# Ring sizes and asking distance of the expert gathers; the last norm's rows moved onto the scores; spread weights read with step zero

## The reference, cut to what matters

```python
hpre = jnp.einsum('tkd,td->tk', u_tab[e_b], x_b)
y = jnp.einsum('tk,tkd->td', g_b * jax.nn.gelu(hpre, approximate=False), v_tab[e_b])
x2 = layer_norm(DN_ALPHA * x1 + y, ln2_g, ln2_b)
```

## Time and profile before

| | us |
|---|---|
| runs, median of 3 | 2384.51 |
| runs, lowest and highest | 2361.98, 2390.08 |
| profiled execution, its own time | 2363.84 |
| its span, first to last instruction | 2362.0 |
| expert loop, first to last dot product | 559.8 to 2333.7 |
| busy share PE, DVE, ACT, POOL | 71%, 58%, 17%, 43% |
| moved by DMA in all | 719.97 MB |
| of it by GpSimd's queue | 556.16 MB |
| mean granted TensorE clock | 0.774 of 2.4 GHz |

### The profile page before, as it was taken

How to read it: one execution, slowest core, us unless ns; L and a number is a source line. 1 busy time by engine, 2 the same in 40 slices (tenths; PEclk the granted TensorE clock), 3 DMA queues, 4 the chain that set the end, 5 groups by cost and what they waited for, 6 DMA issues and landing times. The chain is left out here.

```text
span 2362.0 us, 32086 instructions
## 1 busy us (share of the span) xinstructions
PE 1668.0 (71%) x12789; PEld 1004.3 (43%) x12789; DVE 1362.1 (58%) x2926; ACT 393.5 (17%) x745; POOL 1024.4 (43%) x1094
## 2 busy tenths in 40 slices
PE   7998878874878784787776657867785555555554
PEld 7886756752556451465444324544451001000000
DVE  4394367576444458755434777454457666575744
ACT  1331422131222011123101102320001001000000
POOL 0000200003544445464544545445556666666664
PEclk9997989995999895698887869988886555555555
DMA  9215366427999999699999998999999999999996
GB/s 258 54 36 178 94 160 215 169 89 254 360 356 394 396 370 360 231 348 376 388 385 337 366 352 300 343 354 379 368 389 347 364 354 360 362 369 371 378 370 256
DMA packets 270871, 719.97 MB, mean 305 GB/s; under 512 B 29219, under 2 KB 77822, under 8 KB 269690
## 3 DMA queue, kind: packets, MB, share of 16 engines
q0 software_dynamic: 152336, 556.16, 63.6%
q1 hardware_dynamic: 115736, 160.91, 20.2%
q10 hardware_dynamic: 2650, 0.85, 0.2%
HBM read 696.10 MB, written 21.82 MB: 304 GB/s over the span
## 5 line engine op out<-in xcount | busy, mean ns | idle before, releaser
L2448 DVE CUSTOM_DVE_ANT_0 arena<-arena,ps 128x1024 f32<-128x1024 f32 x520 | 634.4, 1220 | 577.5 <-PE ps L2501 548.5
L2381 POOL DMA_INDIRECT arena<-peer_u_dram,arena x520 | 503.3, 968 | 656.7 <-DVE arena L2448 553.7
L2514 PE MATMUL ps<-arena 128*32 128x512 f32 x2080 | 404.6, 862 | 287.1 <-DMA arena<-peer_v_dram,arena 275.9
L2386 POOL DMA_INDIRECT arena<-peer_v_dram,arena x520 | 491.4, 945 | 166.7 <-issue 152.0
L1291 PE MATMUL ps<-arena 128*128 128x128 f32 (+1 forms) x3072 | 444.8, 303 | 61.6 <-DMA arena<-w_in_dram 29.4
L1291 PEld LDWEIGHTS ps<-arena 128*128 128x128 f32 x3072 | 406.8, 211 | 179.9 <-issue 158.4
L2501 PE MATMUL ps<-arena 48*128 48x512 bf16 x1040 | 260.4, 494 | 262.2 <-DVE arena L2448 242.4
L2501 PEld LDWEIGHTS ps<-arena 48*128 48x128 bf16 x1040 | 53.2, 97 | 544.5 <-DVE arena L2448 384.0
L2514 PEld LDWEIGHTS ps<-arena 128*32 128x32 f32 x2080 | 51.2, 126 | 380.5 <-issue 303.4
L2482 ACT ACTIVATE arena<-arena 128x4 f32<-128x4 f32 x130 | 26.7, 205 | 935.4 <-DVE arena L2448 935.1
L383 PE MATMUL ps<-arena 128*128 128x260 f32 (+1 forms) x704 | 131.0, 348 | 4.1 <-ACT arena L461 4.1
(11 more groups left out here) (363 smaller groups left out, 1830.8 us busy)
## 6 DMA issues: line engine op xcount, KB each, us to landing
arena<-w_in_dram SPq DMA_DIRECT2D x40, 1024.0 KB, 10.9
arena<-peer_wq_dram SPq DMA_DIRECT2D x32, 1024.0 KB, 11.6
arena<-w_out_dram SPq DMA_DIRECT2D x16, 1024.0 KB, 10.5
arena<-w_in_dram SPq DMA_DIRECT2D x30, 512.0 KB, 3.9
arena<-peer_u_dram,arena POOLq DMA_INDIRECT x520
arena<-peer_v_dram,arena POOLq DMA_INDIRECT x520
arena<-w_branch_a_dram SPq DMA_DIRECT2D x8, 1024.0 KB, 10.2
arena<-w_branch_b_dram SPq DMA_DIRECT2D x8, 1024.0 KB, 11.0
```

Of the source, the lines that this page charges most:

```text
L2381: pool.indirect_dma_start(e["U"][:, k % RU, :], None, a["peer_u"][0], offsets(k)).then_inc(u_in[k % RU // UB], 16)
L2386: pool.indirect_dma_start(e["V"][:, j % RV, :], None, a["peer_v"][0], offsets(j)).then_inc(v_in[j % RV // BATCH], 16)
L2448: dve.tensor_tensor_reduce(u, u, ps[:, 0:2, :], 1.0, 0.0, ALU.mult, ALU.add, e["hp"][:, c:c + 1]).then_inc(sem("e_h"), 1)
L2514: mm = pe.matmul(ps[32 * c:32 * c + 32, b + h, :], e["hz"][:, (k + c) % RH, ZW // 2 - r:ZW // 2 - r + 32], e["V"][:, (k + c) % RV, h * 512 ...
```

## The change

The U ring goes from 8 rows to 6, the V ring from 8 to 12, and LAG from 14 steps to 9. `y` lies over the first half of the scores, and `pick` keeps one column for each of the 16 tokens, which TensorE reads 128 times with step zero. The rows of block n-1 are loaded for the norm at step 118 of that block, once the next choice is done, with a semaphore of its own for the sample; scores for block 2 and 3 and for the sample wait until `y` has been saved. The sample's scores go from step 386 to 404, and its choice from 1.5 to 1.2 steps a piece.

```diff
--- before.py
+++ after.py
@@ -145,7 +145,7 @@
     _F_AT[f"s{_g}"], _F_AT[f"se{_g}"] = 74.7 + 4.4 * _g, 75.0 + 4.4 * _g
 BEGINS = (-160.0, 3.0, 106.0, 224.0)
 STRETCH = (1.0, 1.0, 1.3, 1.3)
-CHOOSE_PACE = (0.55, 0.58, 0.78, 0.94, 1.5)
+CHOOSE_PACE = (0.55, 0.58, 0.78, 0.94, 1.2)
 RECUR_SPAN = 31.0
 SLOTS = 3
 
@@ -1395,6 +1395,8 @@
     def scored(g):
         yield front_at(n, f"se{g}")
         wait("s", g + 1)
+        if n > 1 and g == 0:
+            act.wait_ge(m["sem"]("y_saved"), 16 * (n - 1))
         act.activation(d["scores"][:, 4 * g:4 * g + 4].rearrange("p j n -> p (j n)"), ps[:, FB, :], ACT.Copy).then_inc(F_["se"], 1)
 
     yield from gates(0)
@@ -2148,8 +2150,8 @@
             turn_chosen(m, pe, d)
 
 
-RU, RV, RH = 8, 8, 12
-LAG, LEAD = 14, 12
+RU, RV, RH = 6, 12, 12
+LAG, LEAD = 9, 12
 GROUP = 16
 UB = 2
 ZW = 63
@@ -2158,12 +2160,13 @@
 
 def running_buffers(m, space):
     take = space.take
-    m["e"] = dict(U=take([P, RU, D]), V=take([P, RV, D]), hz=take([P, RH, ZW]), pick=take([P, GROUP, P], BF16), pick1=take([P, GROUP]),
+    m["e"] = dict(U=take([P, RU, D]), V=take([P, RV, D]), hz=take([P, RH, ZW]), pick=take([P, GROUP], BF16), pick1=take([P, GROUP]),
                   xp=take([P, 2, 512], BF16), hp=take([P, 2 * GROUP]), hg=take([P, 2, BATCH]), g2=take([P, D]), b2=take([P, D]),
-                  y=take([P, D]), stat=take([P, 4]))
+                  stat=take([P, 4]))
     f = dict(choose={name: take(shape, dt) for name, shape, dt in CHOOSE}, scores=take([P, HP, NK]))
     m["e"]["junk"] = f["choose"]["one"].rearrange("p h i j -> p (h i j)")
     m["finbuf"] = take([P, NFIN * (P + NS)])
+    m["e"]["y"] = flat(f["scores"])[:, 0:D]
     at = space.at
     m["b1"] = {name: take(shape) for name, shape in (
         ("PR", [P, HR, 4, 64]), ("TTr", [P, HR, 64]), ("TMr", [P, HR, 64]), ("Xr", [P, HR, 64]), ("Vt", [P, 512]), ("Kt", [P, 512]),
@@ -2207,7 +2210,7 @@
     return 2 if n < NT else FB
 
 
-SS = 386.0
+SS = 404.0
 
 
 def rows_pe(m, pe):
@@ -2239,6 +2242,7 @@
         yield SS + 0.6 + half
         act.wait_ge(sem("ss_mm"), half + 2)
         act.wait_ge(sem("sel_done"), 2 * NT)
+        act.wait_ge(sem("y_saved"), 16 * (NT - 1))
         act.activation(d["scores"][0:NS, 8 * half:8 * half + 8].rearrange("p (b j) n -> p b (j n)", b=2), ps[0:NS, FB:FB + 2, :], ACT.Copy
                        ).then_inc(sem("ss_out"), 1)
     for q in range(3):
@@ -2321,13 +2325,13 @@
 
     def load_x(n):
         for here, x, _ in rows(n):
-            sp.dma_start(here, x).then_inc(sem("e_x"), 16)
+            sp.dma_start(here, x).then_inc(sem("e_x" if n < NT else "e_xs"), 16)
 
     def save(n):
         sp.wait_ge(sem("e_y"), n + 1)
         for here, _, out in rows(n):
-            sp.dma_start(out, here).then_inc(saved, 16)
-            m["saved"] += 16
+            sp.dma_start(out, here).then_inc(sem("y_saved") if n < NT else saved, 16)
+            m["saved"] += 16 * (n == NT)
 
     yield -2.0
     sp.wait_ge(sem("e_zeroed"), 2)
@@ -2346,12 +2350,12 @@
         if k == 2 * GROUP:
             sp.dma_start(e["g2"], a["ln2_g"].to_broadcast([P, D])).then_inc(sem("e_gb"), 16)
             sp.dma_start(e["b2"], a["ln2_b"].to_broadcast([P, D])).then_inc(sem("e_gb"), 16)
-            load_x(0)
         if s == 2 * GROUP and 0 < n < NT:
             save(n - 1)
-            yield k + 4.0
-            sp.wait_ge(saved, m["saved"])
-            load_x(n)
+        if s == 0 and n:
+            yield k - P + TURN[n - 1] + 2.0
+            sp.wait_ge(sem("sel_done"), 2 * n + 2)
+            load_x(n - 1)
         if s == 6 * GROUP and n == NT - 1:
             sp.wait_ge(sem("x1_saved"), 16 * (13 * NT + 4))
             load_x(NT)
@@ -2359,6 +2363,7 @@
     for n in range(NT - 1, NT + 1):
         save(n)
     sp.wait_ge(saved, m["saved"])
+    sp.wait_ge(sem("y_saved"), 16 * NT)
     sp.wait_ge(sem("states"), 32)
 
 
@@ -2400,7 +2405,7 @@
     dve.memset(e["hz"], 0.0).then_inc(zeroed, 1)
     dve.memset(e["xp"], 0.0).then_inc(zeroed, 1)
     st.link(dve.tensor_tensor(e["pick1"], const(m, "mod16").to_broadcast([P, GROUP]), const(m, "iota16"), ALU.is_equal))
-    dve.tensor_copy(e["pick"], e["pick1"].unsqueeze(2).to_broadcast([P, GROUP, P])).then_inc(zeroed, 1)
+    dve.tensor_copy(e["pick"], e["pick1"]).then_inc(zeroed, 1)
     dve.wait_ge(zeroed, 3)
 
     def norm(n, part):
@@ -2409,7 +2414,7 @@
             if n == 0:
                 dve.wait_ge(sem("e_gb"), 32)
             dve.wait_ge(sem("e_mm"), n * P + count(n))
-            dve.wait_ge(sem("e_x"), 16 * (n + (4 if n == NT else 1)))
+            dve.wait_ge(sem("e_x" if n < NT else "e_xs"), 16 * (n + 1) if n < NT else 64)
             dve.scalar_tensor_tensor(out=two(x), in0=two(x), scalar=ALPHA, in1=ps[:, b:b + 2, :],
                                      op0=ALU.mult, op1=ALU.add).then_inc(sem("e_ff"), 1)
         elif part == 1:
@@ -2498,7 +2503,7 @@
             pe.wait_ge(sem("e_h"), k)
         for h in range(2):
             r = slice(64 * h, 64 * h + 3 * GROUP)
-            mm = pe.matmul(ps[:, h, :], e["pick"][r, i, :], e["xp"][r, g % 2, :], start=True, stop=True)
+            mm = pe.matmul(ps[:, h, :], e["pick"][r, i:i + 1].to_broadcast([3 * GROUP, P]), e["xp"][r, g % 2, :], start=True, stop=True)
         mm.then_inc(sem("e_xb"), 1)
 
     def add_rows(k, h):
```

## The result

The changed kernel takes 2219.51 us (median of four runs, 2209.88 to 2222.21) against 2382.85 for the kernel before (four runs, 2361.98 to 2390.08): a ratio of 0.9306 [0.9269, 0.9344]. The forecast was 2317 us with 2260 as its lower end, so the sign was right and the gain is more than twice what was foretold. The profiled execution took 2219.24 us, its span 2217.4, against 2363.84 and 2362.0: 144.6 us of span.

The account below looks back on a forecast made before the run. The prediction took a closed loop of V asks, sums and dots to bound the kernel, with transfers next: 2363.84 - 53 - 4.5 = 2306.3 us, plus 11 for the profiled execution being fast, forecast 2317 us, range 2260 to 2388.

Parts of the forecast that it names:

- The closed loop: Expert loop: V's ask waits for a dot product that waits on earlier V sums; four steps become seven, opening it.
- What is late next: Expert loop once opened: GpSimd asks (2.48 us a step), transfers (2.65) or U rows; transfers were expected to become the limit.
- The size of the room: Five expert-loop stretches: raising transfers to 395 GB/s would save 105.7 us together; half, 53 us, was taken.
- The halving: Taking 53 of 105.7 us, because no row showed gathers alone at 395 GB/s and DVE's choice falls in lumps.
- The ceiling of 395 GB/s: Best transfer rate in the earlier trace, at 708 to 826 us beside weight transfers, taken as the most the expert loop reaches.
- rival 2: Expert-loop transfers fill all the room up to 395 GB/s: 2264 us, chance 0.13.
- rival 1: Expert-loop transfers are at their limit already, so the wait only moves to U rows: 2370 us, chance 0.28.
- rival 3: Six U rows are too few, dots wait for U, late steps take 3.10 us: slower, 2420 us, chance 0.12.
- The turn of four steps: Late expert loop: one repeat of the chain of waits, 11.34 us before, was to take about 10.9 us.
- The end: After the last dot: four V asks instead of eight follow the last release, so the sample's norm starts 4.5 us earlier.
- The start: Before the first dot: two fewer U rows asked first, V asked 5 steps earlier; nothing taken, 3 us either way.
- What was costed at nothing: Step-zero pick, norm rows over the scores with moved loads and waits, and the sample's later choice: each valued at nothing.

Follow-up runs that it names:

- half V rows: The changed kernel with V gathers of 2 KB instead of 4 KB rows, both halves of the sums using them: 2082.42 us, 0.8766 of the kernel before.
- old rings: The changed kernel with U ring 8, V ring 8 and LAG 14 as before, all else kept: 2371.89 us, 0.9966 of the kernel before.

## Why the prediction was right in kind and wrong in size

*The closed loop: right.* Four steps became seven, the V wait fell from 275.9 to 34.3 us (under 100 was foretold), and the loop's length alone, varied by LAG, moves the time from 3142 to 2209 us.

*What is late next: right.* Of the three candidates it is the transfers, felt at the U rows. A U row may take 11.8 us at 2.65 us a step by the prediction's sum; those on the chain take 10 to 13. That the bytes set the pace is shown by the half V rows, and that V's lead no longer does by LAG 8. A larger U ring beside 12 V rows wasn't tried; that it would give little is argued from the DMA share alone, 1.02 to 1.03 in every stretch that runs at 398 to 403 GB/s.

*The size of the room: wrong, and this is the step that failed.* The prediction says "I take half, 53 us". Measured in the five stretches that it counted: 21.7 + 27.2 + 24.9 + 39.5 + 8.6 = 121.9 us, more than its upper end of 105.7. The halving and the ceiling went into that, and beside them stretches that were counted as nothing.

The ceiling of 395 GB/s was too low: four of the five stretches ran at 398 to 403. With 402 in the same sum the room is 33.4 + 24.4 + 21.5 + 44.9 + 6.5 = 130.7 us, and 121.9 is 0.93 of it.

The halving was the larger part. One of its reasons was that DVE's lumps leave room unfilled. In 1675 to 2101 us DVE is busy 310.89 of 426 us, 73%, and the rate is 403 GB/s; in 2101 to 2177 us it is busy 49%, and the rate is 402. So the lumps cost no transfer time that shows in the rate; that rows in flight carry the engines through a lump is argued, not shown. The other reason was that no row showed gathers alone at 395 GB/s. But the row of 372 GB/s that stood "nearest" had nothing to say of a limit: the late stretch of the run with LAG 12 shows that 363 GB/s at share 0.97 is a loop that waits.

"Nothing is counted in 944 to 1062 and 1400 to 1500" was wrong by 18.2 us. In both stretches TensorE's idle time shrank, from 21 to 17 us and from 18 to 12 (stretch minus busy in the earlier trace rows and after). In the first its busy time fell too, from 97.0 to 89.2 us for as many matmuls, at a mean granted clock of 0.86 instead of 0.82 of full speed (a mean over time at 2.4 and at 1.2 GHz); with four steps in the loop and the clock at 0.75 it was 105.1. That an 82% busy engine on which the sums stand in order still passes on what they wait for fits this, but the size isn't sharp, since executions differ here. With four steps the two stretches took 116.8 and 101.3 us (the kernel before), 125.5 and 107.3 (old rings) and 126.0 and 111.6 (LAG 12), with seven and eight steps 105.9 and 94.0, and 106.0 and 92.0. Against the other two four-step runs the changed kernel gains 33 and 38 us there. Why the clock was granted more often wasn't tried. It isn't what the gain as a whole comes from: in dots 325 to 513 it reads 0.53 and 0.50 before and after, and 48.1 us are gained there.

The sum with the measured terms is 121.9 + 18.2 - 2.1 (last six steps) + 3.1 (start) + 3.6 (end) = 144.7 us in place of 57.5. On the medians the gain is 163 us, since the profiled execution of before was among its fastest. For the same reason the prediction added 11 us to its sum; the profiled execution of the changed kernel, 2219.24 us, stood at its median, and so these 11 us of the miss are not the mechanism's.

*The range.* Its lower end was rival 2, all the room at 395 GB/s. That rival came nearest, but it inherited the ceiling and the uncounted stretches, and so the range ended 40 us above the result. The largest gain should have let the rate go past the best row, as that row was itself no proof of a limit.

*Rivals 1 and 3: fell.* The wait did move to the U rows, but with the rate up from 363 to 403 GB/s and steps of 2.56 to 2.69 us where rival 3 had 3.10. The Trainium skill's rule that rival 1 was weighed with ("DMA: Bandwidth & Descriptors", section "Where 436 GB/s comes from": the memory side, about 358 GB/s a core, binds) doesn't hold as a limit of this kernel: the trace shows 403 GB/s over 426 us, of which the gathers of 158 steps at 1.049 MB are 166 of 171 MB. The Trainium skill's section gets its figure by halving a memory stack's 716 GB/s between two cores. This program runs on one core, and no run here shows a second one at work.

*The turn of four steps.* Foretold 10.9 us at about 380 GB/s; measured 4 x 2.56 = 10.2 at 402, over dots 483 to 513.

*The end: right, slightly less.* 3.6 us instead of 4.5. Four asks follow the release as foretold; the last row took 8.0 us instead of 6.2.

*The start.* 3.1 us earlier, at the edge of the 3 us either way that was allowed.

*What was costed at nothing: right.* The run with the old rings puts all of it together at 0.9966 [0.9923, 1.001]. The spread's weights read with step zero load no slower than those of the earlier trace rows; line L2506 alone, its weight loads (min/median/max ns):

```profile
L2506 PEld LDWEIGHTS ps<-arena x1040: 91/94/200, 555.9 to 2192.0; 48*128 48x128 bf16 x174
```

No group of ACT names a saved y as what it waits for. (The trace has the saves of the prompt's y at steps 145, 272 and 400, about step 16 of a block, as the prediction counts them, and not at step 32.)

## What to carry to other kernels

For a gather that runs ahead of its use, count the steps from the event that lets the ask out (the dot whose slot it queues behind, on its own engine's order) to the first instruction that stands behind its consumer: here that number alone, 10 - LAG + RU, decided between 3142 and 2209 us, and a larger ring without the shorter lag gave nothing (2379), a shorter lag without the larger ring under half. A DMA share of 0.97 is no proof of saturation: look whether the issuing engine waits for the consumers of the same data (553.7 us here), and if so, take the ceiling as unknown upwards. When a loop is opened, don't halve the room without a row that says what stays unfilled (here 0.93 of it at 402 GB/s came), and count the stretches in which another engine is 80% busy as well.

## What was not expected of the hardware

Rows of 4 KB gathered one by one ran, with little beside them, at 402 and 403 GB/s over 1675 to 2177 us, faster than the 395 GB/s of the stretch beside weight transfers in the earlier trace rows. Over 1027 to 1338 and 1432 to 1675 us, where a quarter of the bytes are other transfers (the gathers are 93 of 125 and 72 of 97 MB), it was 401 and 398. The share of the DMA engines read 1.02 to 1.03 in all of these: that, not 0.97, is what full looks like in this table. In dots 483 to 513 the rate rose by 8% (372 to 402), while a row on the chain of waits went from about 6.2 us, ask to landing, to between 10 and 13. What sets the 403 GB/s (the memory, the DMA engines or what they write to) no run here tells.

GpSimd's ask for 128 rows costs the same 0.94 to 0.95 us whether the rows have 4 or 2 KB, so two asks a step take 2 x 1.24 = 2.48 us of it with the 0.30 behind each, less than 0.1 under the 2.56 of the changed kernel's steps 483 to 513. With half V rows the steps 325 to 483 came to 404 / 158 = 2.56 us, and by these numbers fewer bytes still would meet GpSimd there.
